# Recurrence of an RWKV-7 layer on one core: half products over 32 columns instead of 64

## The reference, cut to what matters

```python
def step(state, inp):
    r_t, w_t, k_t, v_t, kk_t, a_t = inp
    sa = jnp.einsum('bhvk,bhk->bhv', state, -kk_t)
    state = (state * w_t[:, :, None, :] + sa[..., None] * (kk_t * a_t)[:, :, None, :]
             + v_t[..., None] * k_t[:, :, None, :])
    return state, jnp.einsum('bhvk,bhk->bhv', state, r_t)
```

## Time and profile before

| | us |
|---|---|
| median of 3 runs | 2545.24 (2544.97 to 2547.05) |
| the profiled execution's own time | 2542.81 |
| its span, first to last instruction | 2541.1 |
| PE busy | 2456.7 (97%) |
| DVE busy | 1084.8 (43%) |
| ACT busy | 478.1 (19%) |
| POOL busy | 179.7 (7%) |

### The profile page before, as it was taken

How to read it: one execution, slowest core, us unless ns; L and a number is a source line. 1 busy time by engine, 2 the same in 40 slices (tenths; PEclk the granted TensorE clock), 3 DMA queues, 4 the chain that set the end, 5 groups by cost and what they waited for, 6 DMA issues and landing times. The chain is left out here.

```text
span 2541.1 us, 80246 instructions
## 1 busy us (share of the span) xinstructions
PE 2456.7 (97%) x36143; PEld 2102.3 (83%) x36143; DVE 1084.8 (43%) x2659; ACT 478.1 (19%) x1061; POOL 179.7 (7%) x226
## 2 busy tenths in 40 slices
PE   9999999999999999999999999989999999999998
PEld 7898877789879989999999898777767777778775
DVE  5682544477321010110101102356765478866666
ACT  2111000111132323210000001220001355542000
POOL 0100000010022222220000000000000001111000
PEclk9999999999999999999999999999999999999999
DMA  7444554554579999999999999435574000020553
GB/s 240 154 146 138 178 161 124 183 168 159 209 290 407 407 407 408 407 407 407 407 408 407 407 407 344 120 106 190 206 235 149 26 9 8 7 71 26 174 179 110
DMA packets 290018, 571.57 MB, mean 225 GB/s; under 512 B 18190, under 2 KB 180244, under 8 KB 289876
## 3 DMA queue, kind: packets, MB, share of 16 engines
q1 hardware_dynamic: 289876, 569.56, 61.5%
HBM read 568.44 MB, written 5.28 MB: 226 GB/s over the span
## 5 line engine op out<-in xcount | busy, mean ns | idle before, releaser
L2688 PE MATMUL ps<-xg,ring 128*64 128x80 f32 x14336 | 506.3, 233 | 7.2 <-issue 5.6
L2688 PEld LDWEIGHTS ps<-xg,ring 128*64 128x64 f32 x14336 | 499.5, 137 | 12.7 <-issue 8.3
L2811 DVE TENSOR_TENSOR hidden<-acted,ps 128x320 f32<-128x320 f32 x64 | 28.5, 446 | 659.9 <-PE ps L2688 659.9
L2704 PE MATMUL ps<-hidden,expert_down 128*64 128x80 f32 x7168 | 258.3, 234 | 9.5 <-DMA expert_down<-in_moe_w_down_dram 4.1
L2704 PEld LDWEIGHTS ps<-hidden,expert_down 128*64 128x64 f32 x7168 | 252.8, 138 | 12.3 <-issue 9.4
L2753 ACT ACTIVATE ring<-second 128x1792 f32<-128x1792 f32 x60 | 101.9, 1698 | 211.4 <-PE ps L2688 156.1
L639 PE MATMUL ps<-xT,ring 128*128 128x256 f32 (+1 forms) x592 | 131.5, 381 | 0.7 <-DMA ring<-in_w_in_dram 0.7
L639 PEld LDWEIGHTS ps<-xT,ring 128*128 128x128 f32 (+1 forms) x592 | 105.9, 181 | 23.9 <-issue 3.5
L2745 POOL COPY ring<-second 128x1792 f32<-128x1792 f32 x60 | 100.9, 1681 | 307.7 <-PE ps L2688 181.9
L639 PE MATMUL ps<-ring,xT 128*128 128x256 f32 (+1 forms) x544 | 108.9, 361 | 2.2 <-PEq L1144 2.2
L639 PEld LDWEIGHTS ps<-ring,xT 128*128 128x128 f32 x544 | 96.0, 190 | 14.5 <-issue 3.0
(11 more groups left out here) (664 smaller groups left out, 3906.6 us busy)
## 6 DMA issues: line engine op xcount, KB each, us to landing
expert_down<-in_moe_w_down_dram SPq DMA_DIRECT2D x96, 1024.0 KB, 17.1
ring<-in_mlp_w_dram SPq DMA_DIRECT2D x64, 1024.0 KB, 5.3
ring<-in_moe_w_gate_dram SPq DMA_DIRECT2D x68, 896.0 KB, 16.0
ring<-in_moe_w_up_dram SPq DMA_DIRECT2D x68, 896.0 KB, 16.7
second<-in_moe_w_gate_dram SPq DMA_DIRECT2D x30, 1792.0 KB, 18.7
second<-in_moe_w_up_dram SPq DMA_DIRECT2D x30, 1792.0 KB, 18.9
ring<-in_w_xkv_dram SPq DMA_DIRECT2D x16, 1024.0 KB, 5.4
expert_down<-in_moe_w_down_dram SPq DMA_DIRECT2D x32, 512.0 KB, 16.3
```

The costliest lines, as they stand in the source:

```text
L2688: mm = pe.matmul(bank[b][o:o + HEAD, at, :], w[:, c, f * P + o:f * P + o + HEAD], xg[:, p * E_STEP + c, :], start=(p == 0 and c == 0 and a ...
L2704: mm = pe.matmul(yT[c // 4][o:o + HEAD, c % 4, :], w[:, j, c * P + o:c * P + o + HEAD], hidden[:, f, :], start=False, stop=False, skip_gro ...
L2811: dve.tensor_tensor(hidden[:, part, :], acted[:, part, :], src, ALU.mult).then_inc(hidden_ready, 1)
```

## The change

`halves` streams only the 32 columns of `XX` that the level changes, and writes them side by side: 32 columns per case, 128 in all. `take_half` copies 128x128 instead of 128x256 and spreads it out in `Pb` to the places that the level changes. What stands in the other places of `Pb` is left from earlier levels, and `steps` still multiplies all 64 columns; those places are masked out by DVE's copy. So that the first level reads no undefined values, POOL clears both `Pb` at the start of the stage, and ACT waits for that once, ahead of its first copy. At level k the changing places come in runs of 2^k elements: 8 bytes at level 1, 16 at level 2, up to one run of 128 bytes at level 5.

```diff
+        PART = HEAD // 2
+
+        def changing(block, k, kind, d):
+
+            return block.rearrange("p (m z b) -> p m z b", z=2, b=1 << k)[:, :, region(kind, d), :]
...
             def _(pool):
+                pool.memset(Pb[0][:], 0.0)
+                pool.memset(Pb[1][:], 0.0).then_inc(self.cleared.sem, 1)
...
                 def take_half(i, k, d):
                     wait(act, "half_done", i, 2 * (k - 1) + d + 1)
-                    act.activation(Pb[d][:].rearrange("p a b -> p (a b)"), ps[:, A(d), 0:4 * HEAD], ACT.Copy).then_inc(q["half_ready"].sem, 1)
+                    to = changing(Pb[d][:].rearrange("p a b -> p (a b)"), k, 0, d)
+                    act.activation(to, ps[:, A(d), 0:4 * PART].rearrange("p (m b) -> p m b", b=1 << k), ACT.Copy).then_inc(q["half_ready"].sem, 1)
...
                     take_m1(0, d)
+                act.wait_ge(self.cleared.sem, self.cleared.at(2))
...
                             h, other = half(b), half(1 - b)
-                            mm = pe.matmul(ps[other, A(d), n * HEAD:(n + 1) * HEAD], GM[d][h, n, 0, h], XX(i, d, 0, n)[h], start=True, stop=True)
+                            mm = pe.matmul(ps[other, A(d), n * PART:(n + 1) * PART], GM[d][h, n, 0, h], changing(XX(i, d, 0, n)[h], k, 0, d), start=True, stop=True)
```

## The result

The changed kernel takes 2554.63 us in the median of 5 runs (2548.55 to 2558.43), the kernel before 2545.24; the ratio is 1.0038, 95% interval 1.0028 to 1.0049. Repeated later on another chip it was 2550.14 against 2543.99, ratio 1.0029 (1.0017 to 1.0042). So it is slower, and it scatters over 10 to 17 us where the kernel before scatters over 5 to 7. The profiled execution took 2551.82 us, its span 2550.1.

The account below looks back on a forecast made before the run. PE was nearest to a bound, but DVE sets much of a middle pair's path. Gains of 0.32 us (middle pairs), 0.55 (first) and 0.30 (last), together 1.2, took the median from 2545.24 to 2544.0 us; range 2538.5 to 2547.5.

Parts of the forecast that it names:

- 27 ns a group of half products: PE's `halves`: each group of eight starts was taken to end 27 ns sooner with 32 moving columns.
- the rival with 13%: PE's `halves`: streaming alone sets the starts, so the kernel gets faster than forecast; range down to 2538.5 us; chance 13%.
- Middle pairs are set by DVE: Middle pairs: only two of ten `halves` lie on the path; savings at the other eight run into waits for DVE.
- The copy, 271 ns: ACT's copy from PSUM: 271 ns instead of 383, hidden in middle pairs; with a strided penalty, 0.49 us at level 1.
- The sum of gains, 1.2 us: Whole recurrence: 0.32 us in six middle pairs, 0.55 in the first, 0.30 in the last, together 1.2.
- Strided reading by PE costs nothing, the clearing costs nothing: PE's level 1 reads in runs of 2 and POOL's two memsets (0.63 us, under cover) were both taken as free.
- The clock: PE's granted clock in the recurrence: the sum held it as before, 1.00 in middle pairs.
- The rival: Thinner PE work lowers the clock once in each of 7 more pairs, up to 10.5 us, 2554.5; chance 7%.
- the sign that the forecast itself named as wrong: Middle pairs: any stretch at a clock below 1 would show the forecast wrong.
- The pause belongs to instruction supply and counts only in the range's ends: Last pair: PE's 2.71 us pause and its slow clock, some 4.2 us together, may move or vanish with small shifts.
- The range: Whole kernel's time: down to 2538.5 us, up to 2547.5, the highest earlier run.

Follow-up runs that it names:

- E9: Changed kernel with each half product cut into two matmuls of 32 weight by 32 moving columns; 2556.47 us in one run.
- e10: Kernel before with each half product cut into two matmuls of 32 weight by 64 moving columns; 2554.83 us in one run.
- e3: Changed kernel with the next feed-forward's first weight loads issued after the last pair's level 5; 2540.73 against 2544.14 us, ratio 0.9986.
- e11: Changed kernel again, without an edit, beside the kernel before on another chip; 2550.14 against 2543.99 us.
- e5: Kernel before with the next feed-forward's first weight loads issued after the last pair's level 5; 2539.32 against 2544.55 us, ratio 0.998.
- e7: Changed kernel with 32 moving columns in the last pair alone, 64 in the other pairs; 2549.67 against 2544.55 us, ratio 1.0017.
- e1: Changed kernel with half products streaming all 64 columns again, short copy and clearing kept; 2544.06 against 2544.14 us, ratio 1.0001.
- e2: Changed kernel with 64 moving columns in the last pair alone, 32 in the other pairs; 2543.06 against 2544.14 us, ratio 1.0.
- e4: Changed kernel with one more matmul a pair in PE's wait for DVE ahead of solve_first; 2549.70 against 2544.14 us, ratio 1.0015.
- e6: Kernel before with ACT's short copy and later weight loads, 64 moving columns kept; 2538.29 against 2544.55 us, ratio 0.9976.

## Why the prediction was wrong

- *27 ns a group of half products.* Right in size. No row or run of before shows the 27 ns that the sum takes; the profile after shows groups 27 ns shorter (medians of 564 and 537 ns from the first start to the next work). They are won at the first start, which the second follows after 31 ns instead of 58; the first record is the shortest, 192 ns, 26 less than the 218 of before. From the last start to the next work it is 155 or 156 ns in both. The trace of before allows an estimate of the same size: a record takes 592 ns with 512 moving columns (L2081) and 275 with 128 (L2046), so 0.83 ns a column, 26 ns for 32 and 53 for 64. What sets the starts: L955 has 128 weight columns, 64 moving ones and a start every (2.44 - 0.275)/19 = 0.114 us, twice the 0.058 of the half products, so an estimate of 57 ns for 64 weight columns. E9 and e10 show both limits (31 or 32 ns with 32 and 32 columns, 55 or 56 with 32 weight and 64 moving). Streaming alone does not set the starts: with half the moving columns they stayed 58 or 59 ns apart but for the first, so the rival with 13% is out.
- *Middle pairs are set by DVE.* Right: 31.51 against 31.53 us, with PE's wait for DVE grown from 0.51 to 0.64 (the forecast had that wait unchanged, and 0.05 us less for the pair). All three dips that the profiles show in middle pairs (pair 5 here and in e3, pair 3 in e11) began within 1.5 us behind this wait.
- *The copy, 271 ns.* Right in size: 278 in the median of a middle pair, with no extra at level 1 (at most 291, where 490 was the bound). The first pair won 0.45 of the 0.55 us forecast.
- *The sum of gains, 1.2 us.* Put together from parts at full clock, one profile each, it comes out: 0.45 in the first pair, some 0.16 in the six middle ones (0.32 forecast), 0.56 in the last (0.30 forecast, e3 against e5). That the total fits so well is partly luck, since two terms are off in opposite ways.
- *Strided reading by PE costs nothing, the clearing costs nothing.* Right: a level 1 group takes 0.59 us to the next work where it took 0.61; POOL's clearing was over by 2041.1 and ACT's first copy began at 2044.53.
- *The clock.* This step failed. The rival was named and given 7%, and the sum held the clock as before. Its mechanism was right, fewer columns and a lower clock, but its price was taken from the wrong quantity. I priced new dips in middle pairs at 1.5 us each, by the length of the one stretch in the earlier trace rows, and left the existing slow stretch at its length. Measured: middle pairs have a dip in each of the two profiles (pair 5 there 1.0 us longer than before, pair 3 in e11), which is the sign that the forecast itself named as wrong. But the larger part, 7.8 of 9.0 us, comes from the stretch that was there already, which grew from some 3.5 us to 23. Once the clock was low, it stayed at 0.50 for 20 to 23 us beside the thinner work (after, e7, e11). E1 (same instructions, 64 columns) has none of it, and e2 and e7 put it into the last pair. Why the chip keeps the clock low there, no run shows. In the forecast's words, what I claimed would speak against the rival, that "the clock is 1.00 in all other stretches", says nothing of a stretch where it already is 0.50.
- *The pause belongs to instruction supply and counts only in the range's ends.* That it is instruction supply fits the DMA records (e5), but it was the trigger of the largest loss. E5 shows that it was worth 5.2 us in the kernel before by itself (4.5 in the last pair of the two profiles), a little over the 4.2 I had put on it.
- *The range* reached to 2547.5 and was too short on the slow side for that reason.

## What to carry to other kernels

In this kernel's float32 products of 64x64 the weight load allowed a start every 58 ns and the stream every 56, and the slower of the two set the rate: halving the moving columns won 0.03 us of 0.57 a group, halving both won 0.18. Where a stage runs beside pauses of TensorE, columns streamed "for nothing" may pay for the clock: before they are removed, look in the profile at how long each existing stretch at half clock lasts, and price the change as if these stretches grew, not only as if new ones came. And look at what shares the time with PE's pauses: issuing four weight loads some 25 us later was worth 5.2 us, where the whole change was forecast at 1.2.

## What the runs showed that was not expected

- TensorE stayed at a granted clock of 0.50 for 20 to 23 us while PE was 97% busy (22.27 of 23.00 us). Here a busy share near one was no sign that the clock returns.
- Four weight loads of 1 MB each, beside the densest matmuls of a stage that needs no weights, went with a pause of 2.4 to 3.0 us in PE's own instructions, in every profile of e1, e2, e4, e7 to e11 and the two kernels; with the same loads some 25 us later, beside thinner work, in e3, e5 and e6, there was none. In the kernel before no 16 KB instruction packet began for 7.4 us while the loads ran; in e5, without them, such packets began 4.5 and 5.9 us apart there.
- ScalarE writing 128 elements in runs of 2 took no longer (258 to 291 ns over all levels) than in long runs, while VectorE's masked copy takes 0.72 us in runs of 2 and 0.40 in runs of 4. PE's moving operand in runs of 2 took no longer either (0.59 us a group of level 1, where contiguous columns took 0.61). Which of the masked copy's operands costs the time isn't shown.
